# Value matmuls of a latent attention: one matmul of 128 stationary columns, or two of 64

## What is computed

```python
def mla_attend(qn, qp, k_nope, kpe, v, mask):
    s = (jnp.einsum('bqhd,bkhd->bhqk', qn, k_nope)
         + jnp.einsum('bqhr,bkr->bhqk', qp, kpe)).astype(jnp.float32) * MLA_SCALE
    if mask is not None:
        s = jnp.where(mask, s, NEG_INF)
    p = jax.nn.softmax(s, axis=-1).astype(v.dtype)
    return jnp.einsum('bhqk,bkhd->bqhd', p, v)
```

## Time and profile before

| | |
|---|---|
| median of 2 runs | 2955.84 us (2952.3 to 2959.37) |
| the profiled execution's own time | 2972.96 us |
| its span, first to last instruction | 2971.2 us |
| mean granted clock of TensorE | 0.961 |
| latent attention, 626 to 1166 us | 540 us |

### The profile page before, as it was taken

The page is one execution under the profiler, slowest core; times in us unless marked ns, Lnnn a source line. Parts: engine busy times, 40 slices in busy tenths (PEclk is TensorE's granted clock), DMA queues, the critical chain, the costliest instruction groups (busy, mean ns, idle before and its releaser), DMA issues.

```text
span 2971.2 us, 43455 instructions
## 1 busy us (share of the span) xinstructions
PE 2822.3 (95%) x13872; PEld 2529.7 (85%) x13872; DVE 1891.9 (64%) x2662; ACT 1317.0 (44%) x2744; POOL 299.9 (10%) x336
## 2 busy tenths in 40 slices
PE   8999879989999998899999999999999999999996
PEld 7899768856666666789999999999999999999996
DVE  6877534556666665577747874478744876458743
ACT  5444235634333343455435544355443644446532
POOL 1111010000000001400020002100021100201002
PEclk9999956979999999999999999999999999999998
DMA  7565551222222323233433443334433353333432
GB/s 219 201 235 202 185 120 51 67 58 53 53 55 52 67 54 106 88 105 113 141 114 102 137 153 111 109 101 142 153 116 104 112 176 111 120 103 113 141 123 74
DMA packets 162016, 344.87 MB, mean 116 GB/s; under 512 B 41636, under 2 KB 105860, under 8 KB 160228
## 3 DMA queue, kind: packets, MB, share of 16 engines
q1 hardware_dynamic: 161892, 343.25, 37.5%
HBM read 288.83 MB, written 55.23 MB: 116 GB/s over the span
## 4 chain that ended last, share of the span: by engine, by line
PE 53%; DVE 2%; issue 2%; ACT 1%; DMA 1%; POOL 1%; POOLq 0%; ACTq 0%; DVEq 0%; SPq 0%
PE mf_acc L1875 52%; DMA mix_w_raw<-in_w_up 1%; DVE mix_w_lo L2028 1%; ACT mix_w_hi L1921 1%; POOL mf_ss L1833 1%; PE mf_st L1913 0%; DVE mf_x L2046 0%; DVE mf_xn L2079 0%; DVE mf_x L2051 0%; POOL mf_y L1858 0%; DVE mix_a_lo L2084 0%; ACT mf_sq L1944 0%; ACT mf_sq L1978 0%; DVE mf_rstd L2063 0%; DVE mf_x L2073 0%
## 5 line engine op out<-in xcount | busy, mean ns | idle before, releaser
L2028 DVE TENSOR_TENSOR mix_w_lo<-mix_w_raw,mix_w_hi 128x1024 fp32r<-128x1024 f32 (+1 forms) x338 | 470.8, 1393 | 556.7 <-ACT mix_w_hi L1921 555.9
L1875 PE MATMUL mf_acc<-mix_a_hi,mix_w_hi 128*128 128x424 f32 (+1 forms) x2016 | 724.3, 359 | 28.2 <-DVE mix_a_lo L2058 8.8
L1875 PE MATMUL mf_acc<-mix_a_lo,mix_w_hi 128*128 128x424 f32 (+1 forms) x2016 | 717.5, 356 | 0.0
L1875 PE MATMUL mf_acc<-mix_a_hi,mix_w_lo 128*128 128x424 f32 (+1 forms) x2016 | 717.3, 356 | 0.0
L1921 ACT ACTIVATE mix_w_hi<-mix_w_raw 128x1024 fp32r<-128x1024 f32 (+1 forms) x338 | 382.2, 1131 | 519.2 <-PE mf_acc L1875 488.4
L1875 PEld LDWEIGHTS mf_acc<-mix_a_hi,mix_w_hi 128*128 128x128 f32 x2016 | 382.1, 190 | 43.6 <-issue 11.8
L1875 PEld LDWEIGHTS mf_acc<-mix_a_hi,mix_w_lo 128*128 128x128 f32 x2016 | 382.7, 190 | 10.6
L1875 PEld LDWEIGHTS mf_acc<-mix_a_lo,mix_w_hi 128*128 128x128 f32 x2016 | 382.4, 190 | 8.9 <-issue 0.7
L1343 PE MATMUL la_sc<-ahead_q,ahead_k 97*128 97x512 f32 (+5 forms) x1008 | 362.7, 469 | 0.0
L1875 PE MATMUL mf_acc<-mf_h_hi,mix_w_hi 128*128 128x424 f32 (+1 forms) x944 | 339.2, 359 | 6.8 <-DVE mix_w_lo L2028 3.8
L1875 PE MATMUL mf_acc<-mf_h_hi,mix_w_lo 128*128 128x424 f32 (+1 forms) x944 | 335.2, 355 | 0.0
(11 more groups left out here) (187 smaller groups left out, 3762.9 us busy)
## 6 DMA issues: line engine op xcount, KB each, us to landing
mix_w_raw<-in_w_up SPq DMA_DIRECT2D x220, 512.0 KB, 3.5
mix_w_raw<-in_w_down SPq DMA_DIRECT2D x80, 704.0 KB, 4.1
pi_w_raw<-in_w_in SPq DMA_DIRECT2D x49, 512.0 KB, 5.8
mix_w_raw<-in_w_out SPq DMA_DIRECT2D x40, 512.0 KB, 3.6
ahead_k<-kn_scr SPq DMA_DIRECT2D x8, 1120.0 KB, 14.6
ahead_q<-qn_scr SPq DMA_DIRECT2D x8, 1056.0 KB, 7.9
pi_x_raw<-in_x SPq DMA_DIRECT2D x4, 1696.0 KB, 11.4
qn_scr<-pi_ring SPq DMA_DIRECT2D x16, 424.0 KB
```

The lines of the kernel that those rows point to most:

```text
L1875: mm = pe.matmul(acc[:, t_bank[0], 0:n], w[:, g, k], x[:, k, 0:n], start=(first and k == 0 and m == 0), stop=(last and k == count - 1 and ...
L2028: dve.tensor_tensor(w_lo[:, g, 0:count], w_raw[:, g, 0:count], w_hi[:, g, 0:count].bitcast(F32), ALU.subtract).then_inc(w_split, 1)
```

## The change

`value_tile` issues two matmuls in place of one, for every tile with 128 keys (41 of 42). The first takes stationary columns 0 to 63 and writes partitions 0 to 63 of `la_ov`; the second takes columns 64 to 127 and writes partitions 64 to 127. Both stream the same moving tile. The semaphore goes up with the second. The tile of 64 keys keeps its single matmul. Nothing else is changed.

```diff
-                pe.matmul(ov[:, (5 * p + pos) % 2, off:n], v[0:keys, p, vt], prob[0:keys, (NKT * p + s) % RING, off:n],
-                          start=(m == 0), stop=(s == last_tile[pos]), skip_group_check=True).then_inc(pv_done, 1)
+                for half in (slice(0, V_DIM), slice(V_DIM, P)) if keys == P else (slice(0, P),):
+                    mm = pe.matmul(ov[half, (5 * p + pos) % 2, off:n], v[0:keys, p, vt, half],
+                                   prob[0:keys, (NKT * p + s) % RING, off:n], start=(m == 0),
+                                   stop=(s == last_tile[pos]), skip_group_check=True)
+                mm.then_inc(pv_done, 1)
```

## The result

The changed kernel takes 3040.64 us (median of 2 runs, 3035.73 to 3045.56) against 2955.84 before, 1.027 times (95% interval 1.020 to 1.035). It is slower by 85 us. Six further runs, timed on one chip beside runs of the kernel before, gave 3074.14 us (3052.16 to 3082.95) against a median of 2958.69, 1.039 times (1.033 to 1.044), 115 us. Medians here are of all executions and the ratios with intervals of those in the faster of two states alone, so the two can differ a little.

What follows compares the result with a forecast made beforehand. PE's streaming was taken to bound the latent attention (540 us). Shape changes 108, late start 16, less 10 absorbed, make 114 us: 3087 for the profiled execution, 3071 against 2955.84; the 8-in-10 range was 3045 to 3300.

Steps and rivals of the forecast that it cites:

- the late start: Value tiles: the second half starts 0.05 us behind the first, its load having 64 columns; 0.05 x 328 = 16 us added.
- The bound: Latent attention, 540 us: paced by what PE streams; more PE work lengthens it almost one for one.
- A column costs two cycles in f32, with 64 columns as with 128; nothing is streamed less: Value matmuls: 0.216 us per record of 256 columns, 236 us in all; halving stationary columns saves 0.
- The halves side by side, out of order: Value tiles: both column halves stream together, as row halves do in the window attention, so the second's streaming adds near nothing.
- The serial rival: Value tiles: halves run one after another, 236 + 108 - 10 = 334 us more, 3290 us; chance 0.20.
- the rival with three slots: Value tiles: records start in program order, three slots in place of two, 118 + 114 = 232 us more, 3189 us; chance 0.22.
- the forecast's own range: 3045 to 3100 us: switches 0.28 to 0.33 us a pair, late start 0.0 to 0.11, times 328; chance 0.40.
- The shape change: Value tiles among full-width matmuls: leaving the full array shape and returning empties the array, 0.33 us each, 328 x 0.33 = 108 us.
- the rival that a column change is free: Join to the score passes: columns change without emptying the array, 16 - 10 = 6 us more, 2962 us; chance 0.08.
- What is absorbed: Latent attention: PE's waits for DVE to free a bank of `la_sx` go, 10 us less.
- What the profile after would show: Signs: score step about 0.4 us later, 64-query stretch about 1.5, last four tiles about 2.5, stage 654 us, little change elsewhere.

Runs made afterwards that it cites:

- one half only: The changed kernel with the second column half left out on all tiles except each unit's first (288 of 328 pairs): 3059.60 us, 1.037 times.

## Why the prediction was right or wrong

The forecast was 3071 us, range 3045 to 3300; measured were 3040.64, just below the range, and 3074.14 in the larger set. The mechanism was right in all its parts. What failed is the size of two terms of the sum, 16 us for the late start where about 2 were measured and 10 us absorbed where 17 were, and a low edge that left absorption and clock out. That 3071 lies so near the 3074.14 of the larger set is luck: a sum 20 us too high met runs at a low clock.

**The bound.** Right. PE is busy for 629.80 of the changed stage's 632 us, and of some 111 us that PE was given (328 x 0.34) only the 17 us in which it had waited for DVE did not lengthen the stage.

**A column costs two cycles in f32, with 64 columns as with 128; nothing is streamed less.** Right: 4.52 - 2.37 = 2.15 us for 1280 columns against 2.16 by the price.

**The halves side by side, out of order.** Right, and it was the choice on which most hung. The serial rival (3290) is excluded by 4.52 against 2.37, the rival with three slots (3189) by the same row, which would be near 3.5. What was transferred from row halves held for column halves that share all their rows. What the Trainium skill (TensorE: Matmul & The Clock Gate, What overlaps and what doesn't) says of loads, that they overlap matmuls only in another row group, is not what this trace shows: the four loads, all on the same 128 rows, lie within 0.20 us, the last two under the first records. What it says of strict order is contradicted only record by record: the second half's first record (1003.195) starts ahead of the first half's second (1003.668), but the two matmuls as wholes start and end in their order.

**The late start.** Wrong size: 0.05 us was taken from the load of the first half, and it measured 0.007 in the trace and not more with one half only; the two halves' loads overlap. 16 us in the sum should have been 2. The bound of nothing at all, which the forecast's own range named, was the nearer one.

**The shape change.** 0.33 us from the sample tile with 64 rows; the full tiles show 0.35 with the late start in it, the narrowest 0.25, perhaps because the smaller loads do give something back there (before, its loads of 128 columns took longer than its records of 64 columns streamed; no run separates this). The rows carried over well from rows to columns, and the rival that a column change is free is excluded, most plainly by the kernel with one half only. Here the trace agrees with the Trainium skill (TensorEngine Tiling (Array Packing), Key Properties), by which a change of the mode drains the engine: the next load waits about 0.1 us past the streaming on either side.

**What is absorbed.** Wrong size. I read the waits of PE's matmuls, 10.2 us. The weight load stands ahead of its matmul and waits first, so the load's row is the one to read: 19.3 us, 2.6 of it left.

With the prediction's own 0.33 for the shape change and these two terms as measured, 328 x 0.337 - 17 = 94 us; the stage shows 93.8.

**The range.** Its low edge, 3045, doesn't follow from its own terms. They are 0.28 us for the switches and no late start: 328 x 0.28 = 92 us, less the 10 absorbed is 82, and 2955.84 + 82 = 3038. Without the 10 it is 3048, and the high edge of 3100 also comes out only without it (328 x 0.44 = 144). So the one term that makes the change cheaper was left out of the range, though the sum has it; 3038 would have held 3040.64. (The sum itself is 3070 for 2955.84 + 114, and the rival at 3189 is 3188.) Nor was there any room for the clock. The kernel before runs at 2938 us with a mean clock of 0.973 and at 2977 with 0.958, so an execution carries some 20 us to either side that no term of the sum holds. The sum was 20 us too high (114 for 94), and two runs at a high clock took off another 10. Either alone would have stayed inside. I had the profile's clock row before me, and the earlier trace rows showed the window attention at half clock; I used it for a price and not for the spread.

**What the profile after would show.** The step at 512 queries grew by 0.35 us for a forecast 0.4, the stretch over 64 queries to 1.40 for 1.5, the last four tiles stayed at 2.37 for 2.5, and the stage is 632 us for 654: each is short by the late start or by what was absorbed. "Outside the stage nothing may differ by more than a few us" was wrong for this pair of profiles, by the 33 us of the window attention, which the kernel before shows between its own two profiles.

## What to carry to other kernels

Splitting a matmul by columns (or rows) doesn't make it slower by itself: f32 halves on different parts of the array ran together, the second 0.007 us behind the first. What costs is the visit: here 0.34 us, or 0.28 after what is absorbed, as often as such a matmul stands among full-width ones, so put matmuls of one shape together, and price a visit with an emptied array on both sides and one uncovered load on each. Where matmuls of half height or width are there anyway, issuing the halves in turn shortens them (2.96 to 2.10 us for sixteen records), but here that gave the whole kernel nothing clear at equal clock. And before a difference of 1% is put down to an edit, compare runs at the same mean clock.

A range has to be added up from the same terms as the forecast, the ones that make the change cheaper too, with the spread of the kernel before on top.

## What the hardware showed that was not expected

- Half-width f32 matmuls overlap even between the two records of one matmul and the next matmul on the other columns: sixteen records in 2.37 us, 1280 columns on each half, which is one half's time.
- The granted clock of one stage differs between executions of one program: in the window attention the kernel before had 0.73 and 0.85, worth 30 us, the changed one 0.75 and 0.86, worth 23. Against the stage's own 94 us, a comparison of two medians of two runs each (85) was 9 us too low, and one of six runs with those beside them (115) 21 too high.
